# Splitting the page loads of the first four sequences into keys and latents in a hybrid decoder step

## What is computed

```python
def mla_attend_sample(qcat, lat, past):
    s_past = jnp.einsum('bqhd,bkd->bhqk', qcat, past) * scale       # keys: latent and rope part
    s_new = jnp.einsum('bqhd,bkd->bhqk', qcat, lat) * scale         # the four new tokens, causal
    p = jax.nn.softmax(jnp.concatenate([s_past, s_new], axis=-1), axis=-1)
    o = jnp.einsum('bhqk,bkr->bqhr', p[..., :P], past[..., :KV_RANK])   # values: the latents
    return o + jnp.einsum('bhqk,bkr->bqhr', p[..., P:], lat[..., :KV_RANK])

past = cache_mla[l, page_table].reshape(Bs, past_len, LAT_DIM)
```

## Time and profile before

| what | value |
|---|---|
| median of 3 runs | 2997.55 us (2990.59 to 3002.01) |
| the profiled execution's own time | 2993.76 us |
| its span, first to last instruction | 2992.0 us |
| busy share of PE, DVE, ACT, POOL | 95%, 60%, 41%, 5% |
| mean granted clock of TensorE | 0.978 of full speed |
| transfers | 326.28 MB, 109 GB/s in the mean |

### The profile page before, as it was taken

How to read it: one execution, slowest core, us unless ns; L and a number is a source line. 1 busy time by engine, 2 the same in 40 slices (tenths; PEclk the granted TensorE clock), 3 DMA queues, 4 the chain that set the end, 5 groups by cost and what they waited for, 6 DMA issues and landing times. The chain is left out here.

```text
span 2992.0 us, 49913 instructions
## 1 busy us (share of the span) xinstructions
PE 2847.3 (95%) x20323; PEld 2691.8 (90%) x20323; DVE 1803.6 (60%) x3013; ACT 1226.5 (41%) x2007; POOL 152.4 (5%) x264
## 2 busy tenths in 40 slices
PE   6999989998999999999989999999989999999997
PEld 5999755898999999999989987559989999999997
DVE  5234644578888885445661346445888888754365
ACT  6223423444444454334452342334444444434253
POOL 0000400000010010000000003000000100000000
PEclk9999999999999999999999989999999999999998
DMA  3101243422222146543221022525222222755331
GB/s 134 43 29 49 96 157 112 176 95 71 70 81 86 66 175 240 183 142 123 97 70 43 15 98 84 175 85 181 67 86 73 78 86 72 254 179 183 135 109 63
DMA packets 133863, 326.28 MB, mean 109 GB/s; under 512 B 9978, under 2 KB 75770, under 8 KB 125442
## 3 DMA queue, kind: packets, MB, share of 16 engines
q1 hardware_dynamic: 133634, 323.09, 31.3%
HBM read 271.74 MB, written 51.31 MB: 108 GB/s over the span
## 5 line engine op out<-in xcount | busy, mean ns | idle before, releaser
L236 PE MATMUL psum<-g_tiles,down_units 128*128 128x352 f32 x1056 | 342.8, 325 | 2.3 <-DVE down_units L2638 2.3
L237 PE MATMUL psum<-g_tiles,down_units 128*128 128x352 f32 x1056 | 339.1, 321 | 0.0
L238 PE MATMUL psum<-g_tiles,down_units 128*128 128x352 f32 x1056 | 338.0, 320 | 0.0
L2863 PE MATMUL psum<-t_high,sum_units 128*128 128x264 f32 x1008 | 286.8, 284 | 0.2
L2864 PE MATMUL psum<-t_low,sum_units 128*128 128x264 f32 x1008 | 286.9, 285 | 0.0
L2865 PE MATMUL psum<-t_high,sum_units 128*128 128x264 f32 x1008 | 286.2, 284 | 0.0
L2350 ACT ACTIVATE down_units<-down_units_raw 128x1408 fp32r<-128x1408 f32 x96 | 132.3, 1380 | 288.3 <-DMA down_units_raw<-w_down_dram 288.3
L2638 DVE TENSOR_TENSOR down_units<-down_units_raw,down_units 128x1408 fp32r<-128x1408 f32 x96 | 155.3, 1622 | 141.4 <-ACT down_units L2350 141.4
L236 PE MATMUL psum<-h_high,mix_weight_parts 128*128 128x352 f32 x576 | 193.7, 336 | 11.2 <-DVE mix_weight_parts L228 8.1
L236 PEld LDWEIGHTS psum<-g_tiles,down_units 128*128 128x128 f32 x1056 | 197.9, 187 | 2.9 <-DVE down_units L2638 2.9
L237 PEld LDWEIGHTS psum<-g_tiles,down_units 128*128 128x128 f32 x1056 | 200.5, 190 | 0.0
(11 more groups left out here) (401 smaller groups left out, 7798.8 us busy)
## 6 DMA issues: line engine op xcount, KB each, us to landing
down_units_raw<-w_down_dram SPq DMA_DIRECT2D x96, 704.0 KB, 4.0
block_units_raw<-w_up_dram SPq DMA_DIRECT2D x40, 768.0 KB, 4.6
g_tiles_raw<-gated_rows SPq DMA_DIRECT2D x38, 528.0 KB, 5.1
mix_weight_stage<-w_in_dram SPq DMA_DIRECT2D x18, 1024.0 KB, 4.8
pages<-cache_dram SPq DMA_DIRECT2D x64, 288.0 KB, 4.5
out_weight_stage<-w_out_dram SPq DMA_DIRECT2D x16, 1024.0 KB, 6.8
out_weight_stage<-w_gate_dram SPq DMA_DIRECT2D x16, 1024.0 KB, 4.8
x<-x_residual SPq DMA_DIRECT2D x9, 1408.0 KB, 12.3
```

Of the source, the lines that this page charges most:

```text
L236: pe.matmul(out, lhs[0], rhs[0], start=first, stop=False)
L237: pe.matmul(out, lhs[0], rhs[1], start=False, stop=False)
L238: return pe.matmul(out, lhs[1], rhs[0], start=False, stop=last)
L2863: pe.matmul(out, w[0], parts[0], start=begin and k == 0, stop=False, skip_group_check=not begin)
```

## The change

The 32 transfers of whole pages of the first group become 32 transfers of keys and, behind all of these, 32 of latents, each set with its own semaphores. `past_scores` waits for the keys of its group; `past_values` now waits for latents in both groups. The semaphores that the second group had used alone count on from the first. What follows in SyncE's queue is unchanged in its order.

```diff
--- before.py
+++ after.py
@@ -1565,7 +1565,7 @@
         smx = take("softmax_rows_s", [P, 4])
         ph, block = st.enter_context(phase(
             nc, s_done=1, masked=1, max_step=1, neg_made=1, exp_done=1, rec_step=1, p_made=1, tr_done=1, pt_made=1,
-            o_done=1, o_used=1, uk_loaded=1, uv_loaded=1, pages_loaded=4, keys_loaded=4, latents_loaded=4, out_loaded=2, out_hi_made=1, out_lo_made=1, heads_hi_made=1, heads_lo_made=1, zeroed=1, ql_done=1,
+            o_done=1, o_used=1, uk_loaded=1, uv_loaded=1, keys_loaded=4, latents_loaded=4, out_loaded=2, out_hi_made=1, out_lo_made=1, heads_hi_made=1, heads_lo_made=1, zeroed=1, ql_done=1,
             q_made=1, new_done=1, new_made=1, past_done=1, past_made=1, row_step=1, sexp_done=1, str_done=1,
             spt_made=1, so_done=1, so_made=1, oT_done=1, oT_made=1, ha_done=1, ha_made=1))
         ps = core.psum
@@ -1585,7 +1585,9 @@
         def _(sp):
             sp.dma_start(ukT[:], core.w_ukT[ds1(l)].rearrange("l p h r -> (l p) h r")).then_inc(ph["uk_loaded"], 16)
             for b in range(4):
-                load_pages(sp, core, b, pages[b], ph["pages_loaded"][b])
+                load_pages(sp, core, b, pages[b], ph["keys_loaded"][b], values=False)
+            for b in range(4):
+                load_pages(sp, core, b, pages[b], ph["latents_loaded"][b], keys=False)
             sp.dma_start(uv[:].rearrange("p k n -> p (k n)"),
                          core.w_ukv[ds1(l), :, 1024:2048].rearrange("l p n -> (l p) n")).then_inc(ph["uv_loaded"], 16)
             sp.wait_ge(ph["past_done"], 2)
@@ -1681,7 +1683,7 @@
                 else:
                     pe.wait_ge(ph["new_made"], gr + 1)
                     for q in range(4):
-                        pe.wait_ge(ph["keys_loaded" if gr else "pages_loaded"][q], 16 * N_PAGES)
+                        pe.wait_ge(ph["keys_loaded"][q], 16 * N_PAGES * (gr + 1))
                 for k in range(4):
                     for q in range(4):
                         s = bank[quarter(q), :].rearrange("p (j n) -> p j n", j=4)
@@ -1709,9 +1711,8 @@
             def past_values(gr, half):
                 if half == 0:
                     pe.wait_ge(ph["spt_made"], 3 * gr + 3)
-                    if gr:
-                        for q in range(4):
-                            pe.wait_ge(ph["latents_loaded"][q], 16 * N_PAGES)
+                    for q in range(4):
+                        pe.wait_ge(ph["latents_loaded"][q], 16 * N_PAGES * (gr + 1))
                 for j in range(4 * half, 4 * half + 4):
                     for q in range(4):
                         pe.matmul(bank[quarter(q), 0:VW], spT[:, j, quarter(q)],
```

## The result

The changed kernel takes 3029.39 us (median of four runs, 3028.80 to 3032.29) against 2997.41 us before. The ratio on record for these runs is 1.0117 with a 95% interval of 1.0101 to 1.0133; the two medians alone stand 1.0107 apart. The profiled execution took 3028.8 us, its span is 3027.0.

What follows compares the result with a forecast made beforehand. TensorE bounds the kernel, fed pages at the pace of SyncE's instructions; layer 0's 18.9 + 2.5 and layer 1's 16.6 + 2.5 make +40.5 us, 3034.3 by profile or 3038 by median; predicted 3036 us, range 3023 to 3048.

Steps and rivals of the forecast that it cites:

- What bounds: TensorE, busy 95% of the span; pages reach it at the pace of SyncE's instructions, 8.57 us per call.
- end within the next call's 4.6 us: Page transfers in SyncE's queue: landings were to be over within the following call's 4.6 us of page-number reading.
- Keys in front: First four's keys, layer 0: wait falls from 4.40 to about 1 us, and a 2.5 us slow stretch goes.
- TensorE's lead: After the first keys: TensorE ahead by up to 5.9 us in layer 0, 0.4 in layer 1, swallowed later.
- Four more calls: SyncE's queue, each layer: 32 more transfers and 32 more page-number reads for the first four's latents, 35.1 us.
- The second four later: Second four's pages in SyncE's queue: later by 18.9 us in layer 0 and 22.6 us in layer 1.
- slow stretch behind the last wait: Behind the second four's latents: TensorE at its lower clock costs 2.5 us per layer, bounds 0 and about 5.
- layer 0's block for the second four: SyncE's 64 page transfers for the second four in layer 0, taken to last 67.55 us as before.
- the lower bound of the sum: 3025 us: no slow stretches (-5), calls at 34.3 (-1.6), layer 0's second four at layer 1's pace (-2.5).
- SyncE's work fits into its pause: Rival, SyncE before the second four: extra calls cost at most 16.2 us (layer 0), 18.5 (layer 1); 2987 to 2994; chance 0.06.
- The cheap split: Rival, SyncE's queue: splitting costs nothing there and only the front's gain is left, 2987.5 us; chance 0.02.
- The clock that stays low: Rival, TensorE behind both standstills per layer: lower clock until the stage is over, 3045 to 3049 us; chance 0.14.

Runs made afterwards that it cites:

- reads-only kernel: Kernel before, with 64 more page-number reads per layer, values unused, put in front of w_uv and no transfer split: 3036.24 us, ratio 1.0130.
- the first experiment: The change, with the first four sequences' page numbers read once and kept in registers for their latents: 2995.81 us, ratio 1.0003.
- sequence-by-sequence kernel: The change, but each sequence's latents follow its own keys instead of all keys going in front: 3044.17 us, ratio 1.0159.

## Why the prediction was right

**What bounds.** The reading that pages come at the pace of SyncE's instructions held. The reads-only kernel lost more than the change (41 us against 32) without touching a transfer, and the change lost nothing once 64 reads were taken out of it. The landings that "end within the next call's 4.6 us" are right for the median of 4.5 us, not for the slowest, 5.7 us in layer 0; with whole pages issued faster they take up to 8.8 us, which suggests that for whole pages the pace is SyncE's only as long as it reads between the issues.

**Keys in front.** The forecast was a first wait of about 1 us in layer 0 with no slow stretch behind it; it is 1.04 us, and the next sixteen wide matmuls take 1.92 us. TensorE's lead, put at up to 5.9 us in layer 0, was swallowed at the second four's keys as forecast. At the first four's own latents TensorE did not wait, also as forecast.

**Four more calls.** Predicted 35.1 us; the rows give 65.47 - 30.54 = 34.9 in layer 0 and 66.34 - 30.55 = 35.8 in layer 1, from the first page transfer to `w_uv`.

**The second four later.** Predicted 18.9 and 22.6 us; measured 19.1 and 23.2, both with the former pause used up. The waits at their keys were to be some 10 to 16 us and are 14.77 and 13.27; those at their latents 1 to 7, and are 4.55 and 3.36.

**What was off.** The forecast for the two layers was 40.5 us and the rows give 34.2; the steps were right, and two terms were mis-sized. The slow stretch behind the last wait was put at 2.5 us in each layer and was 1.5 and 0. And layer 0's block for the second four, taken at the 67.55 us of one execution, took 64.76, with a last landing quicker by 0.8 us; the lower bound of the sum had allowed for the former. The further 3 us down to the 32 by which the medians differ are that of the kernel before, whose profiled execution was quicker than its median.

**The rivals.** That SyncE's work fits into its pause did not happen here, and the first experiment shows that its condition was rightly named: with the numbers kept, the calls cost 18.8 and 17.4 us, a little over the 16.2 that it named for layer 0 and within the 18.5 for layer 1, and the time is that of before, layer 0's lead being spent at the second four's latents as that rival said. The cheap split, 2987.5 us, did not come. The clock that stays low did not come either: the slow stretches end after a few microseconds.

**The two rules of the Trainium skill.** The Trainium skill (Perfetto Trace Analysis, DMA Optimizations) says that splitting may let some transfers start sooner. Here the keys went out in the slots that the whole pages had had, and only landed sooner: the first wait fell from 4.40 to 1.04 us, and the kernel became slower. The other sentence, that the sequencer's time to start a DMA is usually small beside the DMA itself (DMA: Bandwidth & Descriptors, Issuing engines are not separate DMA queues), was called contradicted in the prediction. That reading was wrong: it held the eight issues and reads of a call, 8.57 us, against one landing. For one transfer SyncE spends 1.07 us, 0.5 of it on the issue, and the landing takes 2.2 to 2.6 us. What makes the queue the slower side is that SyncE's turns add up while landings overlap: 64 transfers were issued in 65.43 us, where their landings one behind the other would take some 154, an estimate from 32 times 2.6 and 32 times 2.2.

## What to carry to other kernels

Before a transfer is split, count what each further issue makes its queue do, address reads included, and look in that queue's own list of waits for the pause that can take it: here 35 us of further work met pauses of 16 and 12 us, and the rest, less 6 us of slack in layer 1, came out as waits of the engine that bounds the kernel. A lead won at one wait can be taken back at a later wait on the same queue, as it was in the change and in layer 0 of the first experiment; look at all of them. Where addresses are read from memory, read them once and in a stretch where the queue waits anyway; the kernels that did so were quicker by 0.2% with no split and by 0.3% with it.

## What the runs showed of the hardware

Reading one page number costs SyncE about as much as issuing a transfer with it. From its first transfer on, a block of 64 transfers took 65 us with 56 reads between them (the first eight come ahead of it), 48 to 49 with 24, and 34 to 36 with none: some 0.5 us for each read, and 0.53 to 0.56 for each issue.

How long TensorE runs slowly after a wait does not follow from the length of the wait alone. These windows of the changed kernel begin at the four waits' ends (columns as in the earlier trace rows):

```profile
497.10:501.30 4.20, 4.12 (x33) 1.31 (x33) 0.00 (x0) 0.00 (x0) 0.00 (x0) 0.65 0.34 90
...
531.10:534.50 3.40, 3.36 (x33) 1.59 (x33) 0.00 (x0) 0.00 (x0) 0.00 (x0) 0.55 0.00 0
...
1986.60:1991.80 5.20, 5.14 (x32) 1.57 (x32) 0.00 (x0) 0.00 (x0) 0.00 (x0) 0.51 0.42 113
2020.50:2022.40 1.90, 1.90 (x33) 1.13 (x33) 0.00 (x0) 0.00 (x0) 0.00 (x0) 1.00 0.00 0
```

The clock has two levels, 0.5 (1.2 GHz) and 1.00 (2.4 GHz), so 0.65 in the mean of 4.2 us is 2.9 us at the lower one. Behind 14.77 us TensorE thus ran slowly for some 3 us, behind 13.27 us for some 5, behind 4.55 us for some 3, and behind 3.36 us not at all. In other kernels the sixteen or thirty-two matmuls behind shorter waits were slow: behind 2.20 us they took 3.06 instead of 1.92, behind 3.00 us 3.45 instead of 1.93. Even after 25.88 us, in the sequence-by-sequence kernel, the sixteen wide matmuls take 3.64 us and the sixteen after the next step 1.93 again.
